# The doubling steps of the chunk inverse: the sum (power + identity) kept in SBUF and multiplied once, with ScalarE emptying the banks and VectorE adding the identity

## The reference, cut to what matters

```python
def step(S, inp):
    r_t, w_t, k_t, v_t, a_t, b_t = inp
    sa = jnp.einsum("bhij,bhj->bhi", S, a_t)
    S = S * w_t[:, :, None, :] + sa[..., None] * b_t[:, :, None, :] + v_t[..., None] * k_t[:, :, None, :]
    y = jnp.einsum("bhij,bhj->bhi", S, r_t)
    return S, y
```

## Time and profile before

| what | value |
|---|---|
| median of 3 runs | 1057.34 us (1056.35 to 1060.05) |
| the profiled execution: its time | 1058.24 us |
| the profiled execution: its span | 1056.5 us |
| PE busy | 1041.1 us, 99% |
| DVE busy | 680.1 us, 64% |
| ACT busy | 503.3 us, 48% |
| POOL busy | 356.3 us, 34% |
| granted TensorE clock | 0.998 of full speed |

### The profile page before, as it was taken

One profiled execution on the slowest core, in us unless ns is written; L12 is line 12 of the kernel. 1 busy time (PEld: TensorE's weight loads), 2 busy tenths in 40 slices (PEclk: granted clock), 3 DMA queues, 4 the chain that ended last, 5 costly groups with the idle time before them and its releaser, 6 DMA issues.

```text
span 1056.5 us, 26383 instructions
## 1 busy us (share of the span) xinstructions
PE 1041.1 (99%) x11199; PEld 981.1 (93%) x11199; DVE 680.1 (64%) x1184; ACT 503.3 (48%) x927; POOL 356.3 (34%) x194
## 2 busy tenths in 40 slices
PE   8999999999999999999999999999999999999998
PEld 8998899998998998899999868989999999999998
DVE  5488788787875666785571691657999989500003
ACT  6453533443434566635462543654666665522232
POOL 4431221321321410255232201353544544444450
PEclk9999999999999999999999999999999999999999
DMA  7321221220223343655154874413334334433222
GB/s 228 89 73 42 61 62 44 61 79 24 61 63 101 113 120 121 200 179 178 53 209 143 266 276 140 145 71 112 104 97 121 104 98 120 159 114 103 81 63 82
DMA packets 164061, 120.44 MB, mean 114 GB/s; under 512 B 5336, under 2 KB 153066, under 8 KB 163433
## 3 DMA queue, kind: packets, MB, share of 16 engines
q1 hardware_dynamic: 159979, 108.08, 33.1%
q10 hardware_dynamic: 3974, 10.80, 3.0%
HBM read 111.04 MB, written 8.30 MB: 113 GB/s over the span
## 4 chain that ended last, share of the span: by engine, by line
PE 84%; DVE 9%; ACT 2%; DMA 2%; issue 2%; POOL 0%; DVEq 0%; SPq 0%; ACTq 0%
PE ps L552 36%; PE ps L1808 15%; PE ps L1164 12%; PE ps L534 10%; PE ps L1875 3%; PE ps L574 2%; DVE conv_y L2849 2%; DVE cache L3285 1%; DMA q_bc<-q_scratch 1%; PE ps L1111 1%; DVE ps L3198 1%; PE ps L600 0%; DMA x_tok<-in_x_prompt_dram 0%; PE ps L1101 0%; DMA w_raw<-in_w_gate_up_dram 0%
## 5 line engine op out<-in xcount | busy, mean ns | idle before, releaser
L1000 POOL TENSOR_TENSOR w_lo<-w_raw,w_hi 128x1024 fp32r<-128x1024 f32 (+2 forms) x83 | 193.4, 2334 | 410.8 <-ACT w_hi L592 358.6
L552 PE MATMUL ps<-h_hi,w_hi 128*128 128x260 f32 x748 | 161.8, 298 | 0.9 <-DVE gate_b L3140 0.6
L552 PE MATMUL ps<-h_hi,w_lo 128*128 128x260 f32 x748 | 150.2, 282 | 0.0
L552 PE MATMUL ps<-h_lo,w_hi 128*128 128x260 f32 x748 | 150.2, 282 | 0.0
L592 ACT ACTIVATE w_hi<-w_raw 128x1024 fp32r<-128x1024 f32 (+2 forms) x95 | 91.2, 965 | 73.0 <-PE ps L552 62.1
L552 PEld LDWEIGHTS ps<-h_hi,w_hi 128*128 128x128 f32 x748 | 115.3, 188 | 10.5 <-issue 4.5
L552 PEld LDWEIGHTS ps<-h_lo,w_hi 128*128 128x128 f32 x748 | 115.1, 188 | 0.0
L552 PEld LDWEIGHTS ps<-h_hi,w_lo 128*128 128x128 f32 x748 | 115.1, 188 | 0.0
L2849 DVE SCALAR_TENSOR_TENSOR conv_y<-glu,prm,conv_y 128x512 f32<-128x512 f32 x120 | 104.0, 867 | 2.5
L3183 DVE TENSOR_TENSOR sq_acc<-sq_acc,sq_tmp 128x264 f32<-128x264 f32 (+2 forms) x35 | 28.6, 817 | 114.6 <-ACT sq_tmp L2708 76.0
L1051 POOL TENSOR_TENSOR w_lo<-w_raw,w_hi 128x512 fp32r<-128x512 f32 x36 | 51.6, 1435 | 98.5 <-ACT w_hi L2591 98.5
(11 more groups left out here) (569 smaller groups left out, 3073.1 us busy)
## 6 DMA issues: line engine op xcount, KB each, us to landing
w_raw<-in_w_gate_up_dram SPq DMA_DIRECT2D x44, 512.0 KB, 4.6
w_raw<-in_w_in_dram SPq DMA_DIRECT2D x38, 512.0 KB, 3.7
cache<-in_cache_mem_k_dram SPq DMA_DIRECT2D x16, 512.0 KB, 6.3
w_raw<-in_w_down_dram SPq DMA_DIRECT2D x16, 512.0 KB, 3.5
cache<-in_cache_mem_v_dram SPq DMA_DIRECT2D x14, 512.0 KB, 7.0
w_raw<-in_w_k_dram SPq DMA_DIRECT2D x8, 512.0 KB, 3.7
w_raw<-in_w_v_dram SPq DMA_DIRECT2D x8, 512.0 KB, 3.7
w_raw<-in_w_out_dram SPq DMA_DIRECT2D x8, 512.0 KB, 3.8
```

Source lines behind the costliest of these rows:

```text
L552: mm = nc.tensor.matmul(ps[:, 2 * s + a, 0:width], w[:, k, :], x[:, x0 + k, a * width:(a + 1) * width], start=(first and k == 0 and n == 0 ...
L1000: pool.tensor_tensor(lo[:, 0:kts], w_raw[:, b % RAW_SLOTS, 0:kts], hi[:, 0:kts].bitcast(F32), ALU.subtract).then_inc(w_lo_ready, 1)
```

## The change

The matrix with the identity added is now a buffer of its own, `at_one`, laid over the scratch buffer tmp1. In dbl1 to dbl5 the new XI is one product with `at_one` as weights, and nothing is added in PSUM any more. XI and PW, which had the same weights, are now two products of 64 columns. ScalarE empties everything of dbl0 to dbl4: for each half first AT, over both banks, and it signals this (`powers_out`), then the rest. VectorE waits for the step's products and for that signal, then adds the identity to AT, from SBUF to SBUF. Only in dbl5 do both engines empty PSUM, as before. In dbl0 the two results trade banks.

```diff
+    at_one = tmp1[:, 0:T].rearrange("p (c n) -> p c n", n=HS)
...
-                        small(ps[r, base, HS * j:HS * (j + 1)], big[r, n, AT], big[r, n, PW])
-                        mm = small(ps[r, base + 1, HS * j:HS * (j + 1)], big[r, n, PW], big[r, n, AT])
+                        small(ps[r, base, HS * j:HS * (j + 1)], big[r, n, PW], big[r, n, AT])
+                        mm = small(ps[r, base + 1, HS * j:HS * (j + 1)], big[r, n, AT], big[r, n, PW])
...
-                            width = 1 if d >= 4 else 2
-                            small(region(to, i, h, HS, HS * (1 + width)), big[r, n, AT], big[r, n, HS:HS * (1 + width)],
-                                  stop=False)
-                        for n, h, r, to in some:
-                            mm = small(region(to, i, h, HS, 2 * HS), stack_id[r, :], big[r, n, XI], start=False)
+                            mm = small(region(to, i, h, HS, 2 * HS), at_one[r, n, :], big[r, n, XI])
+                        if d < 4:
+                            for n, h, r, to in some:
+                                mm = small(region(to, i, h, 2 * HS, 3 * HS), big[r, n, AT], big[r, n, PW])
...
                 elif name == "dbl0":
-                    ins = go(big[:, cs, AT], ps[:, base + 1, 0:4 * HS].rearrange("p (c n) -> p c n", c=4), ACT.Copy)
+                    go(big[:, cs, AT], ps[:, base, 0:4 * HS].rearrange("p (c n) -> p c n", c=4), ACT.Copy
+                       ).then_inc(powers_out, 1)
+                    ins = go(big[:, cs, PW], ps[:, base + 1, 0:4 * HS].rearrange("p (c n) -> p c n", c=4), ACT.Copy)
+                elif name == "dbl5":
+                    ins = go(big[:, odds, XI], ps[:, base + 1, :].rearrange("p (i n) -> p i n", i=2)[:, :, XI], ACT.Copy)
                 elif name.startswith("dbl"):
-                    a, b = {"dbl4": (0, 2 * HS), "dbl5": (HS, 2 * HS)}.get(name, (0, 3 * HS))
-                    ins = go(big[:, odds, a:b], ps[:, base + 1, :].rearrange("p (i n) -> p i n", i=2)[:, :, a:b], ACT.Copy)
+                    b = (2 if name == "dbl4" else 3) * HS
+                    go(pairs(big[:, cs, AT]), both(base, 0, HS), ACT.Copy).then_inc(powers_out, 1)
+                    ins = go(pairs(big[:, cs, HS:b]), both(base, HS, b), ACT.Copy)
...
+            def one_added(p, k, cs):
+
+                d = int(STEPS[k][0][3:])
+                dve.wait_ge(powers_out, 10 * p + 2 * d + STEPS[k][1] + 1)
+                return tt(at_one[:, cs], big[:, cs, AT], stack_id[:, :].unsqueeze(1).to_broadcast([P, 4, HS]), ALU.add)
...
                 elif name == "dbl0":
-                    ins = V.tensor_copy(big[:, cs, PW], ps[:, base, 0:4 * HS].rearrange("p (c n) -> p c n", c=4))
+                    ins = one_added(p, k, cs)
+                elif name == "dbl5":
+                    ins = V.tensor_copy(big[:, 4 * q:4 * q + 4:2, XI],
+                                        ps[:, base, :].rearrange("p (i n) -> p i n", i=2)[:, :, XI])
                 elif name.startswith("dbl"):
-                    a, b = {"dbl4": (0, 2 * HS), "dbl5": (HS, 2 * HS)}.get(name, (0, 3 * HS))
-                    ins = V.tensor_copy(big[:, 4 * q:4 * q + 4:2, a:b],
-                                        ps[:, base, :].rearrange("p (i n) -> p i n", i=2)[:, :, a:b])
+                    ins = one_added(p, k, cs)
```

More of the change, by code:

```diff
@@ L419, in hybrid_step_kernel @@
     step_mm, step_v, step_a = sem("step_mm"), sem("step_v"), sem("step_a")
+    powers_out = sem("powers_out")
     def prm_col(name, i):
```

## The result

| | before | after |
|---|---|---|
| median (range), 14 runs each | 1058.38 us (1056.35 to 1061.79) | 1064.03 us (1061.65 to 1069.65) |
| ratio, 95% interval | 1 | 1.0053 (1.0038 to 1.0068) |
| the profiled execution: its time | 1058.24 us | 1061.66 us |
| the profiled execution: its span, granted clock | 1056.5 us, 0.998 | 1059.9 us, 0.997 |

The forecast was 1050.5 us with a range of 1047.5 to 1055.0, and "slower" had a chance of 0.07. The profiled execution of the changed kernel is next to the fastest of its fourteen, so the profiles show 3.4 us of a difference that is 5.65 us between the medians.

The account below looks back on a forecast made before the run. TensorE was taken as the bound, busy all 39.40 us of pair 1's lockstep. Per pair 0.23 + 4 x 0.46 - 0.34 = 1.73 us, four pairs 6.9 us off 1057.34: 1050.4, predicted 1050.5, range 1047.5 to 1055 us.

Parts of the forecast that it names:

- the sum is made at 0.47 + 0.06 + 0.42 = 0.95 us: After a half: AT copied out at 0.47 us, signal 0.06, VectorE's addition 0.42, counted from TensorE's end of the half.
- the addition ends at 2.82 + 0.06 + 0.42 = 3.30: dbl4's second half, counted from dbl4's start: AT out at 2.82 us, signal 0.06, addition 0.42; TensorE can start at 3.36.
- VectorE's queue: VectorE's order of work: additions save 0.84 us per pair, 3.57 us are idle, pushed taps cost nothing.
- 4 x 0.34 = 1.4 us: At dbl5 in each of four pairs TensorE waits 0.34 us for the second half, after ScalarE's late dbl4 copies.
- A group left out is worth 0.115 us: TensorE, dbl1 to dbl5: each half loses two identity groups of 0.115 us, saving 0.23 us a half, 0.46 a round.
- 0.03 us per half against the change at most: TensorE: the wide group of 0.215 us becomes two narrow ones of 0.23 us together; costed at nothing.
- 0.23 forecast: dbl1 saves only its second half's 0.23 us, because TensorE already waits there for VectorE.
- The rule on the bottleneck of PSUM: Skill page: both ScalarE and VectorE should empty PSUM; said to decide at dbl4 alone, at a price of 0.34 us.
- the rounds of dbl2 keep 2.89 us: Sign of being wrong: dbl2 rounds stay at 2.89 us, as groups hold TensorE longer than thought or it waits.
- the other two signs: Signs of being wrong: VectorE has no idle time left before pw, or the stages behind 350 us have grown.
- Rival four: Slower by VectorE's queue: additions waiting for ScalarE hold back taps and pw's additions; 1063.7 us, chance 0.07.
- Rival two: A half's longer way shows in every round, 0.5 us more than added up; time about 1053.3 us, chance 0.14.

Follow-up runs that it names:

- e4: Kernel before plus one unused VectorE addition per pair, both operands in SBUF, between its two dbl4 copies: 1063.46 us, ratio 1.0062.
- e7: Kernel before plus one unused VectorE addition per pair at dbl4, one operand in PSUM and one in SBUF: 1057.3 us, ratio 1.0000.
- e6: Changed kernel with dbl4's identity added straight from PSUM, its power not copied, and two taps moved per pair: 1051.61 us, ratio to before 0.9942.
- e5: Changed kernel with GpSimd's difference that starts at dbl4 held until VectorE's second dbl4 addition: 1059.15 us, ratio to before 1.0023.
- e8: Changed kernel with 35 in place of 27 warm-up transposes on TensorE at the start: 1063.17 us in one execution.
- e1: Changed kernel with ScalarE's split of the next weight block behind dbl4's copies, not ahead of them: 1058.2 us, ratio to before 1.0016.
- e3: Changed kernel where VectorE adds dbl4's identity straight from PSUM and ScalarE then empties XI alone: 1054.83 us, ratio to before 0.9982.
- e9: Changed kernel, GpSimd's difference held behind VectorE's second dbl4 addition, tap between dbl5's copies moved behind them: 1058.35 us, ratio to before 1.0008.

## Why the prediction was wrong

**The step that failed** is "the sum is made at 0.47 + 0.06 + 0.42 = 0.95 us" as it was applied to dbl4 ("the addition ends at 2.82 + 0.06 + 0.42 = 3.30"), together with "VectorE's queue", where the additions again stand at 0.42 us and the whole is cost "at nothing". The 421 ns came from gram_a, where GpSimd was idle (in pair 0 these additions stand at 79.66 and 80.33, its differences at 75.58 and 86.61). At dbl4 the addition starts behind ScalarE's split and so, in each of the four pairs, beside GpSimd's difference. There two additions cost 2.65 us in place of 0.76. The wait ahead of dbl5 is 1.73 to 1.88 us, not 0.34, and it lies ahead of the first half, for which the prediction had the sum ready "just in time". In the account above it takes 8.1 us where the forecast had 4 x 0.34 = 1.4 us: 6.7 of the 6.9 us of gain. The half clock behind it (3.0 us) was in no term of the prediction, and neither were the pauses (1.0 us).

It could have been seen. The kernel before already had the effect in a tap with several SBUF operands; the operation's row for 158 to 163 us (duration ns, least / median / most):

```profile
L2849 DVE SCALAR_TENSOR_TENSOR conv_y<-glu,prm,conv_y x4: 752/752/2723, 157.6 to 160.0; 128x512 f32<-128x512 f32 x4
```

One of four identical instructions took 2.72 us, and GpSimd's difference lay from 159.35 to 162.14. That tap, from 159.97 to 162.69, is the last one ahead of dbl0's copy at 162.73, whose lateness the prediction read and took for the work of ten taps. The Trainium skill, page SBUF — State Buffer, section Who interferes with whom, says it outright: VectorE shares a pair of SBUF ports with GpSimd, as an exclusive lock; a VectorE instruction with two SBUF inputs contends with a GpSimd instruction that reads SBUF, and one with at most one SBUF input does not (outside modes that no run here looked at). The runs agree on both halves, 2.36 against 0.42 us (e4, e7). This rule should have stood where the prediction weighed the one on emptying PSUM.

**Right, within the row's resolution.** A group left out is worth 0.115 us: dbl4 and dbl5 are 0.46 and 0.47 us shorter in e6 (2.72 and 1.54 us against 3.18 and 2.01 in pair 0). In dbl2 and dbl3 it is 0.41 and 0.39 us. The 0.05 us between is what the prediction set to nothing, "0.03 us per half against the change at most": the wide group that became two narrow ones. dbl1 gives 0.19 us (0.23 forecast), because VectorE's taps hold both of its halves, the second now 1.12 us behind the first as forecast. In all 1.92 us a pair without waits, against 2.07 forecast before the 0.34 were taken off.

**Right.** ScalarE carries all the emptying of dbl0 to dbl4 without being waited for on its own account: it runs through both halves of a round without a pause, and is idle for 0.84 us ahead of dbl3 in pair 0, as in pair 1. The rule on the bottleneck of PSUM decided nowhere in the changed kernel: at dbl4, where the prediction put its price at 0.34 us, the longer wait covers it. With GpSimd out of the way (e5) that price appears, 0.35 us in pair 0. So this term was right, and it was not what counted.

**Wrong for another reason.** The prediction's own test, "the rounds of dbl2 keep 2.89 us", would have misled: in pair 1 dbl2 lasts 2.91 us, in pair 0 2.48. The 0.43 us lie within the short products of pair 1, at full clock, where one row of five products takes 0.68 us; the trace marks no wait there. They resemble the "issue" pauses; groups that hold TensorE longer would show in pair 0 too. Of the other two signs neither came: VectorE is idle for 1.87 us ahead of pw in pair 1, and the stages behind the last pair have not grown (+3.6 us there, +3.4 us at the end).

**The rivals.** Rival four named the right queue and the right side, at 0.07, and its 1063.7 us is 0.3 us from the median measured. That is luck, for its mechanism was another: additions that wait for ScalarE, taps pushed by them, and pw's additions late in the end. It spread small delays over ten additions and compared them to VectorE's idle time over a whole pair. The real delay is 1.9 us at one place, where TensorE waits for the addition itself and no idle time elsewhere helps; pw's additions are not late. The rival was to decide from 0.44 us per addition on; the forty additions lost 0.19 us each on average (0.61 in place of 0.42), less than half of that, and the kernel was slower all the same. A mean over a pair was the wrong measure. Rival two put 0.5 us on an addition that "starts behind a tap": in dbl2's second half one does start up to 0.5 us behind its copy, and TensorE, which has the slice to do, doesn't wait for it.

**Open.** In the traces of the kernel after and of e8 all five waits of 1.88 or 1.89 us are followed by half clock, and the three of 1.73 to 1.83 us are not; behind the waits of 0.8 to 1.15 us in e4 and of 1.34 to 1.44 us in e5 and e1 there is none. Whether the length decides was not tested, and no kernel isolates the half clock. The medians differ by 2.2 us more than the profiled executions. The granted clocks of the runs point to the half clock there too: the fourteen of the kernel after have a median of 0.995 and go down to 0.992 in the two longest, the profiled one has 0.997. e8's profiled execution has 0.995 with three stretches at half clock in place of two, so the median execution has about one stretch more. At 1.5 us a stretch that is an estimate of most of the 2.2 us; no trace of a longer execution was taken. The "issue" pauses (0.2 to 1.1 us within the short products) appear in another pair in e8, and not at all in e7, whose TensorE program is that of before. In the kernel after, e3, e5 and e9 the long one (0.78 to 1.05 us) stands at the same product, in dbl3 of pair 1. What causes them was not found.

## What to carry to other kernels

Before an elementwise step is moved from PSUM to SBUF-to-SBUF on VectorE, look up what GpSimd does at that place in the timeline: if both operands are then in SBUF and a long GpSimd instruction is already running there, the step costs the rest of that instruction and most of its own time (here 2.36 us for a step of 0.42). A duration from a group of rows holds only where the neighbours are the same; a form whose mean or maximum lies far above its least (here taps of 0.75 us with one of 2.72) says that such neighbours exist. And cover is local: put the long GpSimd instruction beside a stretch where VectorE is idle or works from PSUM (e3); holding it back only picked another victim here (e5, e1, e9).

## What the hardware showed beyond this

- VectorE's addition of 128x256 took 2.36 us beside a GpSimd difference of 2.38 us with both operands in SBUF, and 0.42 us with one in PSUM. A blocked instruction ended 0.28 us (an addition of 0.42 us), 0.62 us (two, of 0.76 us together) or 0.55 us (a tap of 0.75 us) after GpSimd's end, so hardly any of its work was done in the meantime. Copies from PSUM (0.29 us in e5, 0.41 us in e7) and ScalarE's copies (0.36 to 0.39 us) kept their durations beside it.
- After a wait of 1.88 us TensorE was granted 1.2 in place of 2.4 GHz for about 3 us in two pairs of four, which cost 1.5 us each; the fall came 0.7 and 1.1 us after TensorE had started again. Waits of 1.83 and 1.73 us in the other two cost only themselves.
